# A two-layer diffusion step on one core: the router's order, its counts and the way into each expert

## The reference

```python
def _moe(h, router_w, router_b, exp_gate, exp_up, exp_down):
    logits = (h @ router_w) + router_b
    top_val, top_idx = lax.top_k(logits, TOP_K)            # 2 of 8
    wts = jax.nn.softmax(top_val, axis=-1)
    combine = jnp.sum(jax.nn.one_hot(top_idx, N_EXPERTS) * wts[..., None], axis=-2)
    y = jnp.zeros_like(h)
    for e in range(N_EXPERTS):
        y = y + combine[..., e:e + 1] * _swiglu(h, exp_gate[e], exp_up[e], exp_down[e])
    return y

# in each layer, with shift, scale, gate from silu(cond) @ w_mod + b_mod:
#   x <- layer_norm(ALPHA * x + gate * f(x * (1 + scale) + shift), ln_g, ln_b)
```

## Time and profile before

| what | us |
|---|---|
| median of 3 runs | 1995.89 (1995.82 to 2001.03) |
| profiled execution | 1991.73 |
| its span in the trace | 1991.4 |
| router, gather and the way into expert 0 (957 to 1000) | 43.0, PE busy 24.2 |
| expert 0 from there (1000 to 1229.5) | 229.5, PE busy 207.2, DVE busy 112.6, granted clock 0.95 |
| experts 1 to 7 (1229.5 to 1957.8) | 728.3, PE busy 707.0, DMA share 0.92, 326 GB/s |
| last scatter, norm and output (1957.8 to the end) | 33.6 |

### The profile page before, as it was taken

How to read it: one execution, slowest core, us unless ns; L and a number is a source line. 1 busy time by engine, 2 the same in 40 slices (tenths; PEclk the granted TensorE clock), 3 DMA queues, 4 the chain that set the end, 5 groups by cost and what they waited for, 6 DMA issues and landing times.

```text
span 1991.4 us, 21595 instructions
## 1 busy us (share of the span) xinstructions
PE 1775.7 (89%) x8100; PEld 1457.9 (73%) x8100; DVE 1308.1 (66%) x1589; ACT 1002.2 (50%) x1345; POOL 120.2 (6%) x99
## 2 busy tenths in 40 slices
PE   5899979778999958999699897999999999999994
PEld 4777757557778748887477675878787887878783
DVE  5655366663343356765545545889798888888797
ACT  6653352442223242443143233777777677777671
POOL 1005011130000012001200000000000000000001
PEclk9889978789999979998699898999999999999997
DMA  8642242344334334564045353999989899999792
GB/s 304 214 145 80 70 156 93 137 146 140 122 110 127 113 99 148 173 206 163 2 147 172 126 169 121 355 324 350 333 318 350 307 356 315 364 309 371 266 379 80
DMA packets 198482, 411.13 MB, mean 206 GB/s; under 512 B 12879, under 2 KB 46266, under 8 KB 198330
## 3 DMA queue, kind: packets, MB, share of 16 engines
q1 hardware_dynamic: 195050, 398.20, 58.2%
q0 software_dynamic: 3280, 11.02, 1.7%
HBM read 407.19 MB, written 1.98 MB: 205 GB/s over the span
## 4 chain that ended last, share of the span: by engine, by line
PE 80%; DVE 10%; ACT 4%; issue 3%; DMA 1%; POOL 1%; SPq 0%; DVEq 0%; ACTq 0%; POOLq 0%
PE ps L470 23%; PE ps L472 22%; PE ps L471 22%; DVE w_lo L431 4%; PE ps L1249 2%; PE ps L1222 2%; PE ps L1086 1%; ACT w_hi L425 1%; PE ps L649 1%; PE ps L650 1%; ACT hf L1361 1%; DVE Y L1756 1%; PE ps L677 1%; PE ps L878 1%; PE ps L1190 0%
## 5 line engine op out<-in xcount | busy, mean ns | idle before, releaser
L431 DVE TENSOR_TENSOR w_lo<-raw,w_hi 128x1024 fp32r<-128x1024 f32 (+1 forms) x760 | 904.0, 1232 | 282.4 <-ACT w_hi L425 277.5
L425 ACT CAST w_hi<-raw 128x1024 fp32r<-128x1024 f32 (+1 forms) x760 | 763.9, 1047 | 441.1 <-PE ps L472 382.5
L470 PE MATMUL ps<-w_hi,gT_hi 128*128 128x512 f32 x792 | 318.3, 402 | 30.9 <-issue 26.0
L472 PE MATMUL ps<-w_hi,gT_lo 128*128 128x512 f32 x792 | 312.4, 394 | 0.0
L471 PE MATMUL ps<-w_lo,gT_hi 128*128 128x512 f32 x792 | 311.8, 394 | 0.0
L470 PE MATMUL ps<-w_hi,prodT_hi 128*128 128x512 f32 x528 | 210.6, 399 | 8.8 <-DVE prod_dense L2063 5.2
L472 PE MATMUL ps<-w_hi,prodT_lo 128*128 128x512 f32 x528 | 207.3, 393 | 0.0
L471 PE MATMUL ps<-w_lo,prodT_hi 128*128 128x512 f32 x528 | 207.1, 392 | 0.0
L470 PEld LDWEIGHTS ps<-w_hi,gT_hi 128*128 128x128 f32 x792 | 150.7, 190 | 63.5 <-issue 33.9
L470 PE MATMUL ps<-w_hi,hT_hi 128*128 128x512 f32 (+1 forms) x408 | 167.7, 411 | 9.4 <-DVE hT_lo L1746 4.3
L472 PEld LDWEIGHTS ps<-w_hi,gT_lo 128*128 128x128 f32 x792 | 150.7, 190 | 32.8
(11 more groups left out here) (364 smaller groups left out, 2109.9 us busy)
## 6 DMA issues: line engine op xcount, KB each, us to landing
raw<-in_exp_gate SPq DMA_DIRECT2D x176, 512.0 KB, 5.2
raw<-in_exp_up SPq DMA_DIRECT2D x176, 512.0 KB, 5.1
raw<-in_exp_down SPq DMA_DIRECT2D x176, 512.0 KB, 5.4
raw<-in_w_mod SPq DMA_DIRECT2D x96, 512.0 KB, 4.5
raw<-in_w_in_conv SPq DMA_DIRECT2D x24, 512.0 KB, 6.2
raw<-in_ffn_gate SPq DMA_DIRECT2D x22, 512.0 KB, 4.7
raw<-in_ffn_up SPq DMA_DIRECT2D x22, 512.0 KB, 4.7
raw<-in_ffn_down SPq DMA_DIRECT2D x22, 512.0 KB, 3.8
```

The costliest lines, as they stand in the source:

```text
L425: nc.scalar.copy(w_hi[:, s, cols], raw[:, n % RAW, cols]).then_inc(sem("w_hi_ready"), 1)
L431: nc.vector.tensor_tensor(w_lo[:, s, cols], raw[:, n % RAW, cols], w_hi[:, s, cols].bitcast(F32), ALU.subtract).then_inc(sem("w_ready"), 1)
L470: nc.tensor.matmul(out, a[0], b[0], start=start, stop=False)
L472: return nc.tensor.matmul(out, a[1], b[0], start=False, stop=stop)
```

## The change

1. **Router.** DVE does `posm`, the copy of the counts and `select` right after `H_lo`, one bias add, then a plain cast of the eight counts, and the weights `comb` last of all. The running sums are gone. PE puts one `mod_post` right behind the ranks and one behind `turn_rows`, and waits for the counts only behind these; ACT no longer waits for them ahead of the rows.
2. **Counts in registers.** PE, ACT and DVE each load all eight counts once. The tiles and scatters so far are two more registers, added to at the end of each body.
3. **The bodies' order.** One compare-and-branch leads into the one-tile body, which now stands first; the other two stand behind it. A branch hint at its start (`mark_branch_hint_location`, built as BRANCH_PREFETCH_HINT) names the unconditional jump at its end, over the others.
4. **Empty work left out.** Expert 0 has no scatter of the cleared `y_last` (the semaphores are moved on by empty instructions), POOL no longer clears it, and expert 7 gathers nothing.
5. **X.** The gain and bias rows of the norm ahead of the router are put onto X by DVE: tile 0 ahead of the clearing of Y, tiles 1 and 2 in units 1 and 2 of expert 0. Their two rows get a place of their own.

```diff
-        def routed(eng, e):
-            return (eng.value_load(counts[0:1, 0, e:e + 1], min_val=0, max_val=T_ALL),
-                    ...
+        class Routed:
+            def __init__(self, eng, kind, name):
+                self.counts = [eng.alloc_register(f"{name}_count{e}") for e in range(N_EXP)]
+                self.behind = [eng.alloc_register(f"{name}_{what}") for what in ("tiles", "scatters")]
+                for e in range(N_EXP):
+                    eng.reg_load(self.counts[e], counts[0:1, e:e + 1])
...
+            def by_tiles(self, e, expert):
+                eng.br_lt(count, P + 1, on_true=f"{name}_one{e}", on_false=f"{name}_more{e}")
+                with nc.body(f"{name}_one{e}", valid_engines=[self.kind]):
+                    past = eng.mark_branch_hint_location()
+                    expert(1, e, tiles0, scat0)
+                    self.add(1)
+                    eng.br(f"{name}_next{e}").branch_hint(past)
+                with nc.body(f"{name}_more{e}", valid_engines=[self.kind]):
+                    with eng.If(eng.snap(count, min_val=0, max_val=T_ALL) > 2 * P):
+                        expert(3, e, tiles0, scat0)
+                        self.add(3)
+                    with eng.Else():
+                        expert(2, e, tiles0, scat0)
+                        self.add(2)
+                    eng.nop()
+                    eng.br(f"{name}_next{e}")
+                nc.switch_bb(f"{name}_next{e}")
...
-                    chain(pool.memset(selT[:, 0, :].bitcast(F32), 0.0))
-                    chain(pool.memset(y_last[0].bitcast(F32), 0.0))
-                    pool.memset(y_last[1].bitcast(F32), 0.0).then_inc(sem("yst_lo"), 1)
...
+                    if k == 2:
+                        pool.wait_ge(sem("by_lo"), KD)
...
-                if k < 3:
+                if k < 2:
...
+            mod_post(MOD_LAST[0], (1,))
-            pe.wait_ge(sem("counts_ready"), 1)
...
-            mod_post(MOD_LAST[0], (1,))
             gather(0, 4)
-            mod_post(MOD_LAST[1])
+            mod_post(MOD_LAST[1], (0,))
             turn_rows(0, 4, g_rows)
+            mod_post(MOD_LAST[1], (1,))
+            pe.wait_ge(sem("counts_ready"), 1)
+            route = Routed(pe, mybir.EngineType.PE, "pe")
...
+                if e == 0:
+                    pe.nop().then_inc(sem("y_out"), 6)
...
+                    elif e == N_EXP - 1:
+                        pass
                     elif u == GATHER_AT:
...
+            full_rows(2, 0)
             for m in range(6):
                 nc.vector.memset(Y[:, m // 2, (m % 2) * 512:(m % 2) * 512 + 512], 0.0).then_inc(sem("y_added"), 1)
...
+                    if e == 0 and 1 <= u < TILES:
+                        full_rows(2, u)
```

More of the change, by code:

```diff
@@ L1306, in expert @@
[L1306 to L1318, removed]
@@ L1320, in _ @@
-            total = pe.value_load(counts[0:1, 2, N_EXP:N_EXP + 1], min_val=0, max_val=6 * N_EXP)
+                    turn_selection(bank)
+                    for s in range(1, tiles):
+                        g = tiles0 + s
+                        pe.wait_ge(sem("selT_ready"), g)
+                        gather(g, bank)
+                        turn_rows(g, bank, g_rows_more)
+                        pe.wait_ge(sem("g_hi"), g * 2 + 2)
+                        pe.wait_ge(sem("g_lo"), g * 2 + 2)
+                        turn_selection(bank)
@@ L1321, in _ @@
+                ffn(gT, expert_unit, tiles, e, after_unit=between, after_phase=scatters)
+            for e in range(N_EXP):
+                route.by_tiles(e, expert)
+            total = route.so_far()[1]
             pe.wait_ge(sem("y_added"), total * 6 + 6)
-            pe.wait_ge(sem("g_hi"), 2)
             pe.nop().then_inc(sem("gathers_done"), 1)
@@ L1627, in _ @@
             rows_in(0, 4, g_rows)
-            act.wait_ge(sem("x_full"), 3 * TILES)
             gathered_hi(0, 4, 0)
-            count, tiles0, scat0 = routed(act, 0)
-            for e in range(N_EXP):
[L1633 to L1672, removed]
-                act.nop()
-                if e < N_EXP - 1:
-                    count, tiles0, scat0 = routed(act, e + 1)
@@ new lines, in _, with expert, splits, stage @@
+            act.wait_ge(sem("counts_ready"), 1)
+            route = Routed(act, mybir.EngineType.Activation, "act")
+            def expert(tiles, e, tiles0, scat0):
+                bank = 6 if tiles == 3 else 4
+                if tiles > 1:
+                    selection_in(tiles0, bank, tiles - 1)
+                    for s in range(1, tiles):
+                        g = tiles0 + s
+                        rows_in(g, bank, g_rows_more)
+                        gathered_hi(g, bank, s)
+                        selection_in(g, bank, tiles - 1 - s)
+                def splits(u):
+                    split_in_loop(act, act_split, u, e)
+                    if tiles == 1 and u == 5:
+                        selection_in(tiles0, bank, 0)
+                    elif e == N_EXP - 1:
+                        pass
+                    elif u == GATHER_AT + 1:
+                        rows_in(tiles0 + tiles, bank, g_rows)
+                    elif u == GATHER_AT + 3:
+                        gathered_hi(tiles0 + tiles, bank, 0)
+                def stage(phase, u):
+                    if tiles == 1 and phase == 0:
+                        return
+                    act.wait_ge(sem("w_used"), val(expert_unit(u), FFN_UNITS, e))
+                    for s in range(tiles):
+                        last = phase == 1 and s == tiles - 1
+                        if not last:
+                            act.wait_ge(sem("y_out"), (scat0 + (1 + phase * tiles + s)) * 6)
+                        b = 2 if tiles == 1 else 2 * s
+                        nc.scalar.copy((y_last if last else y_st)[0][:, :, :],
+                                       ps[:, b:b + 2, :].rearrange("p h (a n) -> p (h a) n", a=2)).then_inc(sem("yst_hi"), 1)
+                ffn(expert_unit, tiles, e, splits, stage)
@@ L2242, in _ @@
             mod_out(MOD_LAST[0], (1,))
+            nc.vector.tensor_copy(counts[:, :], R(1)[:, 0, :]).then_inc(sem("counts_ready"), 1)
+            dve.wait_ge(sem("gate_exp"), 1)
+            ex, w1 = small[:, 8:11], small[:, 16:19]
+            chain(ts(w1, ex, 1.0, None, ALU.add))
+            chain(nc.vector.reciprocal(w1, w1))
+            chain(tt(ex, ex, w1, ALU.mult))
+            chain(tt(R(3), R(3), per_tile(w1), ALU.mult))
+            chain(tt(R(5), R(5), per_tile(ex), ALU.mult))
+            chain(nc.vector.memset(comb[:, :, 0:1], 0.0))
```

215 lines of the change are left out of this document (97 added, 118 removed).

## The result

The changed kernel takes 1947.62 us in the median (1940.80 to 1951.47, 4 runs), the kernel before beside it 1995.86 (1994.13 to 2001.03): a ratio of 0.975, interval 0.9716 to 0.9785. The forecast was 1946. The profiled execution took 1945.55 us, its span is 1943.2.

| stretch, us | before | after | e5 |
|---|---|---|---|
| up to the first logits matmul | 937.0 | 935.7 | 935.9 |
| from there to the selection's transposes of expert 0 | 52.9 | 39.3 | 38.2 |
| expert 0 from there | 239.6 | 229.5 | 227.2 |
| experts 1 to 7 | 728.3 | 705.9 | 692.1 |
| rest | 33.6 | 32.9 | 32.9 |

A forecast was written before the change was run, and what follows sets the result against it. PE was taken as the bound, full in one-tile experts and losing time between experts and in the router. Terms −11.9 − 9.1 − 18.5 − 6 − 3.6 = −49.1 from 1991.73, plus 4.2 for the median: 1946, range 1931 to 1970.

The forecast's parts named there:

- Router and way in: From router to expert 0's selection transposes: POOL relieved, DVE work reordered, counts loaded once; −11.9 us, bounds −16 to −7.
- POOL's part: Router: three DVE operations fall to 0.18 us without POOL's on X, 5.9 us less; tile 0 on DVE adds 1.2.
- The first jump: Ahead of expert 0, a new taken jump over the one-tile body, put at 3.8 us.
- Expert 0 to 1: PE's longest gap, 9.9 us, shrinks to some 0.8 as bodies fall through; −9.1 us, bounds −9.9 to −5.
- Expert 7's gather: Last expert: gather and transposes left out; −3.6 us, bounds 0 to −3.8.
- Six boundaries and the clock: Heads between one-tile experts: hinted jump hidden, −18.5 us (−21 to −10); PE's clock behind gaps, −6 (0 to −7.6).
- DVE's chain: DVE's splits and adds behind PE's last matmul, 16.6 us against PE's 16.3; 0.4 us left per boundary.
- the last 4%: Chance left to a boundary going wrong on ACT or DVE, which branch too; price between A and B's worst.
- Rival A: Hint does nothing: full jump at the body's end, gaps of 1.3 us; −39 us, 1957; 14%.
- Rival B: Weight transfers take PE's place as the bound in one-tile experts; 1954, or 1971 at worst; 12%.
- Rival C: Hinted target displaces next code, so packets inside bodies come late; decides from 1.76 us each, 2016; 4%.

The follow-up runs named there:

- e5: Changed kernel with DVE's code moved by never-executed register adds, so every expert's hint stands at place 9 of its 128-instruction piece; 1935.34 us, ratio 0.9705.
- e7: Changed kernel, but X's three tiles get their gain and bias rows from POOL again, DVE's code kept at its old place; 1946.70 us, ratio 0.9757.
- e1: The changed kernel run again unaltered, as the measure for the runs beside it; 1947.08 us, ratio 0.9751.
- e3: Changed kernel, but DVE's hint alone given in unit 29 of 33, about ten instructions ahead of the jump; 1970.21 us, ratio 0.9871.
- e11: Changed kernel with DVE's hints of experts 1 to 6 moved to places 36, 41, 45, 48, 57, 60; one run, 1961.92 us.
- e8: Changed kernel, but expert 7 again gathers the rows of a ninth expert; 1951.11 us, ratio 0.9780.
- e9: The kernel of e5 once more (DVE's hints at place 9), as the measure for runs beside it; 1939.39 us, ratio 0.9727.
- e12: Changed kernel with DVE's hints of experts 1 to 6 moved to places 64, 70, 80, 105, 125, 25; one run, 1939.08 us.
- e2: Changed kernel with the branch hint left out on PE, ACT and DVE; 1968.50 us, ratio 0.9854.
- e6: As e5, but with every expert's DVE hint at place 51 instead of 9; 1967.71 us, ratio 0.9850.

## Why the prediction was right, and where it was not

*The time* came out 1.6 us from the forecast, the profiled execution 46.2 us shorter (48.2 by the spans) where the sum gave 49.1. Errors of opposite sign are in it: the six boundaries and the clock gave 6 us less than forecast, the head and expert 0 2.7 more, and 2 us come from the first and the last stretch of the table, for which the sum has no term. That the total fits this closely is in part luck.

*Router and way in*, −11.9 forecast: from the first logits matmul to the selection's transposes 52.9 became 39.3, −13.6 in this trace; 38.2 to 41.0 in the ten traces with the same way in, 40.5 in the median, which is −12.4. POOL's part is shown by e7, 5.1 us at `select` against a term of 4.6. `select` came 9.2 us earlier by the logits (8.6 forecast). The first jump, which I put at 3.8, took 5.06 here, and 3.48 to 3.64 in e1 to e3. The sum lets the gather start 0.8 us behind `select`, though it names 1.1; 0.8 is what the trace gives. What I had not counted is the clock in the gather. Its first three matmuls took 2.27 us before; they took 0.94 or 0.95 here and in e5 and e11, and 1.62 in the other ten traces. The granted clock over the gather's start is 0.50, the lower of TensorE's two levels, in the kernel before and in e1, and 1.00 in this trace (columns as in the earlier trace rows; before, after, e1):

```profile
967.20:970.20 3.00, 3.00 (x8) 2.01 (x7) 0.69 (x1) 0.00 (x0) 0.00 (x0) 0.50 0.00 0
...
956.44:957.90 1.46, 1.46 (x6) 1.22 (x7) 1.31 (x7) 0.00 (x0) 0.00 (x0) 1.00 0.00 0
...
957.65:960.31 2.66, 2.66 (x6) 2.12 (x7) 1.54 (x9) 0.00 (x0) 0.00 (x0) 0.50 0.00 0
```

From the gather to the first load it is 4.9 us here and 7.7 in e1, where I had put 7.9; the longer first jump takes part of that back. So the term was right for the lower clock, and what this execution has beyond it is luck. What let the clock rise in three traces, no run separates.

*Expert 0 to 1*, −9.1: PE's gap of 9.91 is 1.10, −8.8.

*Expert 7's gather*, −3.6: 4.0 by e8.

*Six boundaries and the clock*, −18.5 and −6: this is the term that was wrong in its size. With the other terms taken out, experts 1 to 7 gave 22.4 − 4 = 18.4 of the forecast 24.5. I wrote that with the hint "nothing of it is left to see" and left 0.4 us per head for DVE's chain. On PE that held at all heads (0.3 us a jump). I had not carried it to DVE's own jump: DVE branches too, has no lead, and at two heads its hint is lost. Such a boundary stands in the prediction only among the last 4%, and the sum has no term for it. e5, in which no hint is lost, gives those stretches 36.2 us less than before, e9 and e12 33.6 and 34.8; less the gather's 4, that is 30 to 32 where 24.5 were forecast. So without the lost hints the step was too cautious, and the 0.4 us left for DVE's chain is not seen either: e5 has no gap over 0.5 us at a head.

*Rival A* (the hint does nothing) was priced at 10 us above the forecast; e2 gives 21 above e1. The same omission: the rival prices PE's jump alone, and e3 shows that DVE's, at four heads more, costs 23. *Rival B* (weights): no. The DMA share rose to 0.98 and 350 GB/s at 99.3 us per expert in e5, above the 341 I took for the best stretch; ACT's waits for landings of the up-projection rose only from 10.2 to 13.3 us (21.3 in e9, which is faster all the same), and PE waits for none. *Rival C* (code fetched late inside a body): no trace has gaps inside its bodies that come near its price of 1.76 us each, 28 times. The largest of PE's "issue" gaps there are 1.17 us in e2, 0.82 in e7 and 0.56 in e9, one in each trace and within 5 us of a head. The wait that did come stands behind DVE's jump; that it is for the target's code is an inference, as no view names what a code packet holds.

## What to carry to other kernels

Price a branch on every engine that takes it, and first on the one without a lead: here DVE, whose last operation of a body waits for ACT's result, stood idle for 3.6 to 4.8 us behind its jump wherever the hint was lost. Moving work that is fixed at run time (counts, loads, a likely body) off the head of a loop body is worth at most what that head's slowest engine waits; in these traces that wait stands as "issue". Where code is large and branches are hinted, look at each head for a single engine's "issue" waits that return at the same heads in every run; a shift of the code by some instructions may remove them, as it did here for a further 8 to 12 us (e5 and e9 against e1).

## What the runs showed of the hardware that I had not expected

A hint given at the start of a body was kept or lost as a whole on DVE, by the place of the code alone: lost at eight places from 36 to 60 of 128, kept at ten others, and lost six times out of six when it was given about ten instructions, and 13.5 us, ahead of its jump. Where it was kept, DVE took 1.9 us from its jump to the compare at the next head, at every such head of seven traces (the changed kernel's, e1, e5, e7, e8, e9 and e12); where it was lost, 4.1 to 6.1 us, which is no better than without a hint (5.3 to 6.0 in e2). One lost hint on DVE cost 3.6 to 4.8 us there where the trace names "issue", 2.3 to 3.8 us of PE (once, in e7, 0.8), and with the clock at 0.98 behind the gap some 5.4 to 5.9 us of the whole (e6 against e5, e1 against e5).
